# The samples' key and value compression of an attention layer, regrouped: two sequences at a time, over five steps

## The reference

```python
def compress(x, pe, w1, w2):      # x: tokens of one sequence, for each of 2 groups
    # window i covers tokens 16 i .. 16 i + 31: 127 windows of 2048 tokens
    # hidden = gelu(flatten(window_i + pe) @ w1)     (2048 -> 128)
    # out    = hidden @ w2                           (128 -> 64)
    ...
kc = compress(full[:, :, 0], W['pe_cmp'][0], W['w_cmp1'][0], W['w_cmp2'][0])
vc = compress(full[:, :, 1], W['pe_cmp'][1], W['w_cmp1'][1], W['w_cmp2'][1])
n_sel = -(-L // SEL_BLOCK)
o_cmp, imp = compressed_attention(qb, qpos, kc, vc, n_sel)
idx, ok = select_blocks(imp, qpos, n_sel)
o_slc = selected_attention(qb, qpos, to_blocks(full[:, :, 2], n_sel), to_blocks(full[:, :, 3], n_sel), idx, ok)
```

## Time and profile before

| | us |
|---|---|
| median of 3 runs | 1243.46 |
| lowest, highest | 1242.87, 1243.95 |
| the profiled execution, device time | 1244.62 |
| its span, first to last instruction | 1242.80 |
| PE busy | 1214.7 |
| DVE busy | 693.1 |
| ACT busy | 324.8 |
| POOL busy | 281.0 |

### The profile page before, as it was taken

One profiled execution on the slowest core, in us unless ns is written; L12 is line 12 of the kernel. 1 busy time (PEld: TensorE's weight loads), 2 busy tenths in 40 slices (PEclk: granted clock), 3 DMA queues, 4 the chain that ended last, 5 costly groups with the idle time before them and its releaser, 6 DMA issues.

```text
span 1242.8 us, 19650 instructions
## 1 busy us (share of the span) xinstructions
PE 1214.7 (98%) x6846; PEld 952.0 (77%) x6846; DVE 693.1 (56%) x1524; ACT 324.8 (26%) x736; POOL 281.0 (23%) x444
## 2 busy tenths in 40 slices
PE   7999999999999999999999999999999999999999
PEld 6887656878778667666787886787888888888887
DVE  6856354665555451151387715359777888863331
ACT  3422522454454422121121016222112121210000
POOL 5541002333433523332340100221010010100000
PEclk9999999999999999999999999999999999999999
DMA  6532474232334799897513630122222222402240
GB/s 231 201 125 85 144 271 172 83 92 69 103 103 137 222 357 339 287 362 245 223 35 119 245 127 18 51 68 81 85 74 85 85 85 85 140 22 93 93 160 18
DMA packets 83636, 174.59 MB, mean 140 GB/s; under 512 B 11377, under 2 KB 49074, under 8 KB 82642
## 3 DMA queue, kind: packets, MB, share of 16 engines
q1 hardware_dynamic: 67810, 123.79, 29.7%
q10 hardware_dynamic: 11568, 39.06, 8.5%
q0 software_dynamic: 4160, 10.49, 2.5%
HBM read 163.21 MB, written 10.09 MB: 139 GB/s over the span
## 4 chain that ended last, share of the span: by engine, by line
PE 91%; DVE 5%; ACT 2%; issue 2%; DMA 1%; POOL 0%; ACTq 0%; DVEq 0%; SPq 0%; POOLq 0%
PE ps L2963 20%; PE ps L3000 11%; PE ps L1865 10%; PE ps L661 7%; PE ps L1333 6%; PE ps L2674 6%; PE ps L2775 4%; PE ps L754 3%; PE ps L2687 3%; PE ps L1238 2%; PE ps L1266 2%; PE ps L1252 2%; PE ps L650 1%; PE ps L2823 1%; PE ps L653 1%
## 5 line engine op out<-in xcount | busy, mean ns | idle before, releaser
L2963 PE MATMUL ps<-arena 128*128 128x272 f32 x1120 | 257.1, 392 | 0.7 <-DVE arena L3332 0.7
L2963 PEld LDWEIGHTS ps<-arena 128*128 128x128 f32 x1120 | 212.7, 190 | 45.0 <-DVE arena L3332 1.1
L1865 PE MATMUL ps<-arena 128*128 128x272 f32 x512 | 121.9, 395 | 0.5 <-PE ps L1965 0.5
L3000 PE MATMUL ps<-arena 128*128 128x272 f32 x528 | 121.8, 392 | 0.0
L1865 PEld LDWEIGHTS ps<-arena 128*128 128x128 f32 x512 | 95.8, 190 | 27.0 <-issue 8.3
L3000 PEld LDWEIGHTS ps<-arena 128*128 128x128 f32 x528 | 100.3, 190 | 20.7
L1333 PEld LDWEIGHTS ps<-arena 128*128 128x128 f32 x768 | 89.8, 195 | 12.1 <-issue 11.2
L1333 PE MATMUL ps<-arena 128*128 128x128 f32 (+1 forms) x768 | 95.4, 282 | 2.0 <-DVE arena L1460 1.8
L661 PE MATMUL ps<-arena 128*128 128x272 f32 x392 | 91.4, 394 | 0.0
L661 PEld LDWEIGHTS ps<-arena 128*128 128x128 f32 x392 | 74.1, 190 | 16.5 <-issue 1.5
L2622 ACT ACTIVATE arena<-arena 128x560 f32<-128x560 f32 x44 | 35.3, 848 | 159.7 <-DVE arena L3347 152.9
(11 more groups left out here) (396 smaller groups left out, 1860.7 us busy)
## 6 DMA issues: line engine op xcount, KB each, us to landing
arena<-in_w_close SPq DMA_DIRECT2D x68, 512.0 KB, 3.5
arena<-in_pages_cmp SPq DMA_DIRECT2D x128, 128.0 KB, 2.1
arena<-in_past_va ACTq DMA_DIRECT2D x6, 2048.0 KB, 12.7
arena<-in_w_down SPq DMA_DIRECT2D x16, 704.0 KB, 6.0
arena<-in_past_ka ACTq DMA_DIRECT2D x6, 1792.0 KB, 11.5
arena<-in_w_close ACTq DMA_DIRECT2D x16, 512.0 KB, 7.0
arena<-in_w_proj SPq DMA_DIRECT2D x15, 512.0 KB, 3.6
arena<-in_pages_ks SPq DMA_DIRECT2D x96, 64.0 KB, 3.9
```

The lines of the kernel that those rows point to most:

```text
L1865: last_one = pe.matmul(ps[:, gate_bank(q), 0:HALF], ring[:, n % CLOSE_RING, k * P:(k + 1) * P], m.h[:, k, half * HALF:(half + 1) * HALF], ...
L2963: last = pe.matmul(ps[:, bank(f, i), 0:HALF], w[:, k * P:(k + 1) * P], halved[:, rhs, k, :], start=(k == 0), stop=(k == 3))
L3000: last = pe.matmul(ps[:, down_bank(i, j), 0:HALF], w[:, k * P:(k + 1) * P], rhs[:, k, :], start=(k == 0), stop=(k == KH - 1))
```

## The change

The unit of the samples' compression is now a pair n of two sequences with one kv, eight units in all in place of sixteen, with matmuls of 256 columns (252 for BOTH) in place of 128 (126). So each weight is loaded for twice the columns. A unit's three products are spread over five steps (`PIECES`): five eighths of EVEN, the rest of EVEN, five eighths of ODD, the rest of ODD with a quarter of BOTH, the rest of BOTH. ODD is now added onto EVEN in the same place of PSUM. So the even sum is copied out by ACT between them (`take_even`, one step after the start), and POOL forms differences of neighbours from it (`slopes`); `take_first` writes the even-numbered windows by one ACT operation (EVEN + ODD + bias), and `add` on DVE is two operations on 252 elements in place of three. `bend`, the tanh and `hidden` work on all 508 windows of a unit at once; `bend` on ACT comes after `take_turned`. `hidden` stands at the head of its step on DVE, ahead of `add`, `evict` and `weigh`. `small(s)` follows four and five steps after the last product of its sequences, one in each of two steps.

The sums on POOL are cut in four operations for the first part and two for the second, on two sequences. Their result lies in another place, 45820, so the first one waits for `h_scaled`, and the constants of `attend_sample` that lay there are loaded later (`load_constants` moves behind the last product, ahead of `load_masks`). Pages are loaded in halves by kv: 32 transfers of 64 KB for each unit, 256 in all, with 512 bytes in a row; the page table is read once for two units, ahead of the wait. The weights `w1` are issued ahead of the first pages and of the stores. In `attend_sample` SP's wait for the products of sequence 6 becomes one for the last but one unit, and the wait for those of (7, 0) goes. FILL is one step later.

```diff
+    chunked, next_sum = at(37944, 2, 8, 66), at(45820, 16, 2, 64)
     w_both = at(43772, 2, 8, P)
     c_prob_t, c_score = at(39000, 2, T), at(40024, QT, 8, 32)
-    second, inner, bent = at(41048, 2, 2, P), at(41560, 2, 2, P), at(42072, 2, 2, P)
-    hid = at(42584, 2, 2, 2, P)
+    even, slope = at(41048, 4, 64), at(41304, 4, 64)
+    inner, bent = at(41560, 4, P), at(42072, 4, P)
+    hid = at(42584, 2, 4, P)
     table = m.table
...
-    def first_step(s, kv):
-        return 4 + (2 * s + kv) * 5 // 2
-    def last_step(s, kv):
-        return first_step(s, kv) + 1
-    def seq_step(s):
...
+    EVEN, ODD, BOTH = range(3)
+    PAIRS = [(q, kv) for q in range(NSEQ // 2) for kv in range(2)]
+    UNIT_STEPS = 5
+    PIECES = [[(EVEN, 0, 5)], [(EVEN, 5, 8)], [(ODD, 0, 5)], [(ODD, 5, 8), (BOTH, 0, 2)], [(BOTH, 2, 8)]]
+    def begin(n):
+        return 4 + UNIT_STEPS * n
+    def even_step(n):
+        return begin(n) + 1
+    def last_step(n):
+        return begin(n) + UNIT_STEPS - 1
+    def small_step(s):
+        return last_step(2 * (s // 2) + 1) + 4 + s % 2
+    def product_done(n, product):
+        return 1 + 3 * n + product + 1
     def products(s, kv):
-        return 1 + 2 * (2 * s + kv) + 2
-    assert last_step(NSEQ - 1, 1) < STEPS - 4
+        return product_done(2 * (s // 2) + kv, BOTH)
+    assert last_step(len(PAIRS) - 1) < STEPS - 6
...
+    def slot(product):
+        at_ = 256 * (product == BOTH)
+        return ps[:, PROJ, at_:at_ + 256].rearrange("p (x i) -> p x i", x=4)
+    def page_view(n):
+        return pages[:, n % 2].rearrange("p n (a w i) -> p w a n i", a=16, w=2)
+    def windows(kv):
+        return hid[:, kv].rearrange("p x (i w) -> p w x i", w=2)
...
+                found += four
+            return found
+        def load_pages(n, found):
+            _, kv = PAIRS[n]
+            for c, page in enumerate(found):
+                sp.dma_start(pages[:, n % 2, c, :],
+                             d["pages_cmp"][ds(page, 1), :, P * kv:P * kv + P].rearrange("a p n -> p (a n)"))\
+                    .then_inc(page_in[n % 2], 16)
...
-        load_pages(0)
+        found = pages_of(0)
+        sp.wait_ge(m.tile_done, m.NJOB)
+        sp.dma_start(w1, d["w_cmp1"]).then_inc(w_in, 16)
+        load_pages(0, found)
         m.store_tiles(sp)
-        sp.dma_start(w1, d["w_cmp1"]).then_inc(w_in, 16)
         m.store_values(sp)
-        load_pages(1)
+        load_pages(1, found)
         sp.wait_ge(m.stored, 16 * 7)
         sp.wait_ge(m.h_scaled, QT + 1)
-        m.load_constants(sp)
-        for s in range(2, NSEQ):
-            sp.wait_ge(proj_full, products(s - 2, 1))
-            load_pages(s)
+        for n in range(2, len(PAIRS)):
+            if n % 2 == 0:
+                found = pages_of(n // 2)
+            sp.wait_ge(proj_full, product_done(n - 2, BOTH))
+            load_pages(n, found)
...
-            pool.tensor_tensor(to[:, :, 0:NPAGE - 1, 3], x[:, 0, :, 1:NPAGE, 0], x[:, 1, :, 0:NPAGE - 1, 3],
-                              ALU.add).then_inc(chunked_ready, 1)
-        sums(*HALVES[0])
+        def sums(n):
+            pool.wait_ge(page_in[n % 2], 16 * 2 * NPAGE * (n // 2 + 1))
+            if n == 0:
+                pool.wait_ge(m.h_scaled, QT + 1)
+            else:
+                pool.wait_ge(proj_full, product_done(n - 1, BOTH))
+            x = page_view(n)
+            to = next_sum.rearrange("p a s (n i) -> p a (s n) i", i=4)
+            for a in range(0, 16, 4):
+                rows = slice(a, a + 4)
+                pool.tensor_tensor(to[:, rows, :, 0:3], x[:, 0, rows, :, 1:4], x[:, 1, rows, :, 0:3], ALU.add)
+            by_seq = x.rearrange("p w a (s n) i -> p w a s n i", s=2)
+            to = next_sum.rearrange("p a s (n i) -> p a s n i", i=4)
+            for a in range(0, 16, 8):
+                rows = slice(a, a + 8)
+                last = pool.tensor_tensor(to[:, rows, :, 0:NPAGE - 1, 3], by_seq[:, 0, rows, :, 1:NPAGE, 0],
+                                          by_seq[:, 1, rows, :, 0:NPAGE - 1, 3], ALU.add)
+            last.then_inc(chunked_ready, 1)
+        def slopes(n):
+            pool.wait_ge(second_ready, 2 + 2 * n + 1)
+            if n >= 1:
+                pool.wait_ge(proj_free, 2 + n)
+            pool.tensor_tensor(slope[:, :, 0:63], even[:, :, 0:63], even[:, :, 1:64], ALU.subtract)\
+                .then_inc(slope_ready, 1)
         for kv in range(2):
             bend(p_hid[:, kv, :, 0:C], p_inner[:, kv, :, 0:C], kv + 1)
-        for n, (s, kv) in enumerate(HALVES):
-            if n + 1 < len(HALVES):
-                sums(*HALVES[n + 1])
-            bend(hid[:, s % 2, kv, :, 0:NCMP_S], inner[:, kv, :, 0:NCMP_S], 2 + n + 1)
+        sums(0)
+        for n, (q, kv) in enumerate(PAIRS):
...
-            act.wait_ge(inner_ready, 2 + 2 * s + kv + 1)
-            act.activation(bent[:, kv, :, 0:NCMP_S], inner[:, kv, :, 0:NCMP_S], ACT.Tanh, scale=GELU_IN)\
+        def take_even(n):
+            act.wait_ge(proj_full, product_done(n, EVEN))
+            if n >= 1:
+                act.wait_ge(slope_ready, SLOPE0 + n)
+            act.copy(even[:, :, :], slot(EVEN)).then_inc(second_ready, 1)
+        def take_first(n):
+            q, kv = PAIRS[n]
+            act.wait_ge(proj_full, product_done(n, BOTH))
+            if q >= 1:
+                act.wait_ge(s_full, s_index["small", 2 * q - 1] + 1)
...
-                               ODD: (w1[:, kv, 1, s1, :], x[:, 1, s1], part(ODD))}[product]
-                last = pe.matmul(out, w, rhs, start=(s1 == 0), stop=(s1 == 7))
-            if product != EVEN:
+        def piece(n, product, from_, to):
+            q, kv = PAIRS[n]
+            x = page_view(n).rearrange("p w (e s) n i -> p w s e n i", e=2)
+            follows = next_sum.rearrange("p (e s) q i -> p s e q i", e=2)
+            if from_ > 0:
+                pass
+            elif product == EVEN:
+                pe.wait_ge(proj_free, 2 + n)
+                if n >= 1:
+                    pe.wait_ge(second_ready, 2 + 2 * n)
+                pe.wait_ge(page_in[n % 2], 16 * 2 * NPAGE * (n // 2 + 1))
+            elif product == ODD:
+                pe.wait_ge(second_ready, 2 + 2 * n + 1)
+            else:
+                pe.wait_ge(chunked_ready, 10 + n + 1)
+            for s1 in range(from_, to):
+                if product == BOTH:
+                    out = slot(BOTH).rearrange("p (e q) i -> p e q i", e=2)[:, :, :, 0:63]
+                    last = pe.matmul(out, w_both[:, kv, s1, :], follows[:, s1, :, :, 0:63], start=(s1 == 0), stop=(s1 == 7))
+                else:
+                    last = pe.matmul(slot(product), w1[:, kv, product, s1, :], x[:, product, s1],
+                                     start=(product == EVEN and s1 == 0), stop=(s1 == 7),
+                                     skip_group_check=(product == ODD))
+            if to == 8:
                 last.then_inc(proj_full, 1)
         def small(s):
             b, n = s_slot(("small", s)), NCMP_S
...
-            step.wait()
-            dve.tensor_tensor(between, between, part(EVEN)[:, :, 1:64], ALU.subtract).then_inc(proj_free, 1)
+        def add(n):
+            q, kv = PAIRS[n]
+            between = windows(kv)[:, 1, :, 0:63]
+            dve.wait_ge(second_ready, 2 + 2 * n + 2)
+            dve.wait_ge(slope_ready, SLOPE0 + n + 1)
+            if q >= 1:
+                dve.wait_ge(s_full, s_index["small", 2 * q - 1] + 1)
+            step.done(dve.scalar_tensor_tensor(out=between, in0=slot(BOTH)[:, :, 0:63], scalar=m.cmp_bias[:, kv:kv + 1],
+                                               in1=slope[:, :, 0:63], op0=ALU.add, op1=ALU.add))
+            step.wait()
+            dve.tensor_tensor(between, between, slot(ODD)[:, :, 0:63], ALU.subtract).then_inc(proj_free, 1)
...
-                for kv in range(2):
-                    if last_step(s, kv) + 1 == t:
-                        add(s, kv)
+            for n in range(len(PAIRS)):
+                if last_step(n) + 2 == t:
+                    hidden(n)
+            for n in range(len(PAIRS)):
...
-        sp.wait_ge(m.proj_full, m.products(NSEQ - 2, 1))
+        sp.wait_ge(m.proj_full, m.products(NSEQ - 1, 0))
         for c in range(4):
             load_pages(sp, SP, 0, c, 0, "pages_ks", None if c < 2 else early_in[c - 2])
-        sp.wait_ge(m.proj_full, m.products(NSEQ - 1, 0))
         for c in range(2):
             m.load_chunk(sp, c)
         sp.wait_ge(m.s_full, m.last_dilated_scores)
@@ -1683,6 +1736,7 @@
         for c in range(4):
             load_pages(sp, SP, 0, c, 1, "pages_ks", None if c < 2 else early_in[c - 2])
         sp.wait_ge(m.proj_full, m.products(NSEQ - 1, 1))
+        load_constants(sp)
         load_masks(sp)
         m.load_chunk(sp, 2)
```

More of the change, by code:

```diff
@@ L1007, in attend_prompt @@
             s_users.append(("cmp", 0))
-        s_users += [("small", s) for s in range(NSEQ) if seq_step(s) + 3 == t]
+        s_users += [("small", s) for s in range(NSEQ) if small_step(s) == t]
```

(25 more changed lines are left out.)

119 lines of the change are left out of this document (45 added, 74 removed).

## The result

The kernel before took 1243.16 us (median of 4 runs, 1241.98 to 1243.95), the changed one 1259.57 us (median of 4, 1253.11 to 1260.57). The medians are 16.4 us apart, 1.3%; the ratio of the measurement is 1.011, with a 95% interval of 1.0094 to 1.0127. So the change makes the kernel slower by some 1.1 to 1.3%, outside the forecast's range, on its slow side. The profiled execution of the changed kernel took 1260.57 us, its span is 1258.7 us, 15.9 us more than before.

What follows compares the result with a forecast made beforehand. PE, 98% busy, was taken as the bound. Products (2.8 us) and waits (1.3 us) would gain, but late second keys turn this into +0.2, plus 1.6 for the clock: +1.8 on 1243.46, 1245.3 us; range 1239.0 to 1250.5.

Steps and rivals of the forecast that it cites:

- what decides: Sample stage: SP's gapless queue sets when the second keys land; cover 0.65 us before; PE would wait over 3 us.
- the half clock: PE behind the wait for the second keys: granted clock falls from 2.4 to 1.2 GHz, adding 1.6 us.
- the products: Compression on PE: half the weight loads, same columns; 0.35 us saved a pair, 2.8 us over eight pairs.
- The estimate from the Trainium skill's figures: Compression products on PE: 256 columns at about 98 ns, some 40% or over 30 us less; given no chance.
- the page loads: SP's queue in the compression: 256 issues instead of 128, keeping pace with some 3 us to spare; cost nothing.
- the waits of the stage: PE's waits in the prompt stage: 3.1 us until step 38 against 4.4, a gain of 1.3; bounds 1 and 7.
- the even copy: PE's odd products wait for ACT's copy: about 1.0 to 1.1 us at pairs 2 and 6, elsewhere 0.2.
- rival (3): Prompt stage: PE, ACT and DVE at one pace, pairs waiting at EVEN and ODD; 1252 us, chance 0.13.
- `add`: PE's waits for DVE's `add`: three old ones of 1.8 us gone, about 0.8 us new at pair 4.
- (1): Second keys late for PE in the sample stage: range -3 to +7 us, 1240.5 to 1250.5; chance 0.5.
- the trigger: End of pair 6 in step 38, starting SP's sample-stage pages: at 378.2 us, 1.3 earlier than before.
- the landing: Second keys' transfer: 9.2 us after issue plus 1.4 us for sharing the engines, landing at 440.5 us.

Runs made afterwards that it cites:

- experiment 7: Kernel of experiment 5, with the first pair's even product whole in step 4 (16 records in place of 10): 1244.12 us, ratio 1.0007.
- experiment 9: Kernel of experiment 5, with POOL's sums uncut, one operation for each of the two loops: 1265.78 us, ratio 1.0177.
- experiment 10: Kernel of experiment 7, with ACT's copy of the even sum ahead of the step's exponentials: 1240.33 us, ratio 0.9975.
- experiment 11: Kernel of experiment 10, with POOL's sums cut in eight and four operations, not four and two: 1238.42 us, ratio 0.9959.
- experiment 5: Changed kernel, SP's first sample-stage pages waiting for pair 6's odd product and sums, not its product of both: 1246.65 us, ratio 1.002.
- experiment 4: Changed kernel, with the two constants issued behind the second keys, not ahead of the masks: 1257.14 us, ratio 1.0113.
- experiment 6: Kernel before, with the two constants loaded ahead of the masks, in SP's chain to the second keys: 1244.06 us, ratio 1.0003.
- experiment 8: Kernel of experiment 5, with `hidden` back at the end of DVE's step and the small products a step earlier: 1251.07 us, ratio 1.0058.
- experiment 2: Kernel before, with the second keys issued ahead of the last sixteen pages on SP's queue: 1243.68 us, ratio 1.0002.
- experiment 3: Kernel before, with SP's first sample-stage pages waiting for the scores of step 39 instead of an earlier product: 1256.57 us, ratio 1.0093.
- experiment 1: Changed kernel, with the second keys issued ahead of the last sixteen pages on SP's queue: 1255.78 us, ratio 1.0099.

## Why the prediction was wrong, point by point

**Right: what decides.** The forecast named the second keys, their cover of 0.65 us, SP's queue without a gap, and the half clock behind a wait. All of it is in the profile. From trigger to issue I had 51.8 us; it is 386.57 to 439.81, 53.2 us. The half clock was priced at 1.6 us and cost 1.5 us, but that the two agree is luck: the price came from a block worked wholly at half clock, and the stretch here lasted 10.2 us, in most of which PE stood idle. The direction was given 0.36, no more, since the sizes came out small.

**Right: the products.** 384 records in place of 768, and 0.35 us a pair forecast. By the starts of its blocks, each to the start of what follows, a pair costs 10.74 us; by those of the kernel before (385.42 to 389.10 and 377.40 to 379.29, twice) 11.14 us: 0.40 us saved, 3.2 us in eight pairs. Time went by columns, as the rows said. The estimate from the Trainium skill's figures for the gap between matmuls (TensorE: Matmul & The Clock Gate, Back-to-back issue gap) was over 30 us, 40% of the products; the trace of the changed kernel contradicts it for these float32 blocks, with 0.40 of 11.14 us, as that of before did.

**Right: the page loads.** PE waits for no page of the compression.

**Wrong: the waits of the stage, the step that failed first.** I summed them to 3.1 us against 4.4, a gain of 1.3; until 382 us they are 9.0 us, past the 7 us that I had named as a sign of being wrong. PE's gaps of over 0.15 us between 214 us and the keys are 10.3 us against 5.6, a loss of 4.6, and two half clocks of 3.4 us against one add 1.7 us. Together with 0.3 us of a later start, less 3.2 us from the products, that is 3.4 of the 4.5 us by which PE comes late to the keys; the rest stays unexplained. Three terms were missing or small. First, the head: the old step 4 had 32 records of cover, the new one 10, so PE caught up with ACT and DVE, 1.1 and 1.4 us. I compared whole pairs and never the single step. Experiment 7 shows it for the first of the two; the second wait stayed. Second, the even copy: I had 1.0 to 1.1 us at pairs 2 and 6 and 0.2 elsewhere; it is 1.35 and 1.57 us there and 4.1 us in all. The chain was the one described, and from the start of evict to the end of the copy it takes 3.1 us at pair 6 (369.71 to 372.82), less than the 3.7 I had; but its evict is late, since POOL's sums hold two DVE operations before it. I took a hold to be "at most" one part of the cut sum; the six parts follow each other without a pause, and hold one DVE operation after another. That was rival (3), priced at 1252 us, with a chance of 0.13 on the strength of busy shares; DVE's busy share of 0.61 hid that it was the pace in single steps. Experiments 9 and 10 show it from both sides: 19 us for longer parts, 3.8 us for taking the copy out of the chain; the 1.9 us for shorter parts (experiment 11) point the same way and are not clear of the noise. Third, `add`: 1.4 us in three waits, where I had 0.8 us at pair 4 and had put the old 1.8 us down as gone. Two sums of the rivals were also off, by little: (1)'s own bounds add up to +8.6 us, not +7, and (3)'s to some 1253 us.

**Wrong: the trigger.** 378.2 us forecast, 386.4 us measured. The equality of work that I used (before, the end of the scores of step 38) holds; what was put into it did not. The waits of 4.6 us more instead of 1.3 us less, 1.7 us for the second half clock and 0.3 us of a later start make 7.9 of the 8.2 us. The larger omission was in design, not in arithmetic: I took the end of the pair as what frees its pages. Experiment 5 shows that this was some 7 us of waiting for a product that reads no pages, worth 12.9 us.

**Mis-sized: the landing.** I had 9.2 us and 1.4 for sharing, 10.6; it is 14.6 us. The kernel before issued the windows' values at 435.30, the second keys at 430.32 and the third keys at 437.41 us; the changed one issued them at 439.65, 439.81 and 441.76, three transfers of 4608 KB in all in 2.1 us. At the 303 GB/s of the stage that would be some 15.6 us. But this is not shown to be the cause: no run changed the overlap alone, and the other runs do not order by it. The landing was 7.2 to 9.8 us in experiments 4, 5, 6, 8, 10 and 11, 10.3 to 11.4 in 2, 7 and 9, where PE did not wait for the keys either, 11.5 in experiment 3, and 16.2 in experiment 1, where behind the keys no other large transfer was issued for 16 us. What makes a landing of these keys long stays open.

**The constants**, 0.9 us, were rightly sized, and alone without a price.

**The sum** that follows from the runs: prompt stage +4.5 (forecast -4.1), keys' wait +9.8 (forecast 4.3, from an arrival 4.1 us earlier, +0.2 net), half clock +1.5 (+1.6). It is the keys' landing that sets the time: I had PE take them at 440.5 us, and it took them at 454.45 us. These 14.0 us are 8.2 us of the trigger, 1.4 us of the chain from there to the issue and 4.0 us of the landing; the 0.4 us left over are rounding and the choice of where a block ends. That PE itself came 8.6 us later than forecast cost nothing further, as it fell into the wait for the keys. So the steps that failed are two: the trigger, through the waits of the stage, and the landing; the first has its cause shown in the main, the second has not.

## What to carry to other kernels

Before a transfer chain is moved with the work that triggers it, ask for each member who the last reader of its buffer really is; a wait on the whole product where its first part would do cost 12.9 us here. When work is spread more evenly over steps, compare the single steps with the other engines' work in them, not the totals: the step that lost its cover (2.5 us, experiment 7) and the copy that stood behind the exponentials (3.8 us, experiment 10) had cost more than the 3.2 us that the products gave. And an engine at 0.6 of its time can set the pace of single steps, above all where a second engine holds it.

## What the runs showed that I had not expected

A trigger 6.6 us late cost 13.4 us: SP's chain grew by 3 us, most of it in a single issue of a mask (5.10 us for 2.54), the landing by 2.3 us, and the half clock lasted 17 us with PE at work in it. And the same half clock costs from 1.5 us, where PE is idle for most of it, to some 7 us, where it is not (experiment 3: its profiled execution is 14.1 us longer than that of before, of which 7.3 are waits). The length of POOL's operations mattered more than their sum: the whole of them takes longer when cut, `hidden` has a median of 2.37 us beside parts of up to 3.8 us, 1.49 us in the changed kernel and 0.82 us with the finest cut, and the kernel's time follows, 1265.8, 1246.7 and, with the copy ahead, 1240.3 and 1238.4 us, the last step within the noise.
